# Output projection of a streaming encoder layer: whole-array matmuls split into an upper and a lower half of 64 rows

## The reference

```python
h = rms_norm(x, norm_pre)
p = h @ w_in                      # queries, keys, values, gates of three kinds of heads
o = concat(o_A * silu(g_A), o_B * silu(g_B), o_C * silu(g_C))   # "mixed", width 2048
y = x + rms_norm(o @ w_out, norm_post)   # w_out is 2048 x 2048
```

## Time and profile before

| | |
|---|---|
| median of three runs | 1939.62 us (1938.63 to 1939.85) |
| span of the profiled execution | 1936.8 us |
| the profiled execution's own time | not listed apart from the three |
| PE busy | 1905.3 us, 98% |
| DVE busy | 1240.0 us, 64% |
| ACT busy | 666.4 us, 34% |
| granted TensorE clock, mean | 0.997 |
| matmuls L1204 to L1206, 128x352 | 2688 each |
| matmuls L1400 to L1402, 128x512 | 448 each |
| matmuls L1396, L1397 | 64 each |

### The profile page before, as it was taken

The page is one execution under the profiler, slowest core; times in us unless marked ns, Lnnn a source line. Parts: engine busy times, 40 slices in busy tenths (PEclk is TensorE's granted clock), DMA queues, the critical chain, the costliest instruction groups (busy, mean ns, idle before and its releaser), DMA issues.

```text
span 1936.8 us, 30940 instructions
## 1 busy us (share of the span) xinstructions
PE 1905.3 (98%) x12508; PEld 1746.7 (90%) x12508; DVE 1240.0 (64%) x2224; ACT 666.4 (34%) x1257; POOL 53.3 (3%) x119
## 2 busy tenths in 40 slices
PE   6999999999999999999999999999999999999997
PEld 5999999999999999999999999999999988888886
DVE  7358777787878778553544454355525566766878
ACT  7124233343433334222222222233213354344453
POOL 4000000000000000000000000000000000000131
PEclk9999999999999999999999999999999999999999
DMA  6456777676777767666657667465446657555396
GB/s 245 117 120 137 159 157 165 145 147 154 146 162 154 162 146 149 151 137 136 149 119 155 141 136 143 104 141 123 106 97 144 136 197 278 192 175 187 121 258 226
DMA packets 880407, 301.05 MB, mean 155 GB/s; under 512 B 618504, under 2 KB 845592, under 8 KB 878968
## 3 DMA queue, kind: packets, MB, share of 16 engines
q1 hardware_dynamic: 877192, 290.35, 61.6%
q0 software_dynamic: 3072, 8.73, 2.2%
HBM read 210.45 MB, written 96.20 MB: 158 GB/s over the span
## 4 chain that ended last, share of the span: by engine, by line
PE 86%; DVE 9%; DMA 1%; ACT 1%; issue 1%; POOL 0%; SPq 0%; DVEq 0%; ACTq 0%; POOLq 0%
PE ps L1204 21%; PE ps L1205 20%; PE ps L1206 20%; PE ps L1400 4%; PE ps L1401 4%; PE ps L1402 4%; PE ps L1292 3%; PE ps L1371 3%; PE ps L1264 2%; PE ps L1342 2%; DVE arena L1853 1%; DVE act_lo L1740 1%; DVE arena L1733 1%; DMA b_out<-in_w_out_dram 1%; DVE arena L1841 1%
## 5 line engine op out<-in xcount | busy, mean ns | idle before, releaser
L1204 PE MATMUL ps<-act_hi,w_hi 128*128 128x352 f32 x2688 | 878.8, 327 | 0.1
L1206 PE MATMUL ps<-act_hi,w_lo 128*128 128x352 f32 x2688 | 863.7, 321 | 0.0
L1205 PE MATMUL ps<-act_lo,w_hi 128*128 128x352 f32 x2688 | 863.6, 321 | 0.0
L1204 PEld LDWEIGHTS ps<-act_hi,w_hi 128*128 128x128 f32 x2688 | 505.2, 188 | 24.7 <-issue 20.7
L1205 PEld LDWEIGHTS ps<-act_lo,w_hi 128*128 128x128 f32 x2688 | 506.1, 188 | 0.0
L1206 PEld LDWEIGHTS ps<-act_hi,w_lo 128*128 128x128 f32 x2688 | 504.9, 188 | 0.0
L1501 ACT ACTIVATE w_hi<-w_raw 128x512 fp32r<-128x512 f32 x224 | 139.3, 623 | 340.5 <-DMA w_raw<-in_w_in_dram 340.4
L1748 DVE TENSOR_TENSOR w_lo<-w_raw,w_hi 128x512 fp32r<-128x512 f32 x224 | 150.9, 675 | 51.5 <-ACT w_hi L1501 51.2
L1568 ACT ACTIVATE arena<-arena,small 128x257 f32<-128x257 f32 (+6 forms) x180 | 101.3, 565 | 209.1 <-DVE small L1891 209.1
L2079 DVE STREAM_TRANSPOSE arena<-arena 128x1024 f32<-128x1024 f32 (+4 forms) x100 | 132.6, 1326 | 40.0 <-ACT arena L1691 39.2
L1691 ACT ACTIVATE arena<-arena 128x1024 f32<-128x1024 f32 (+1 forms) x60 | 61.0, 1017 | 255.8 <-DVE arena L1865 255.7
(11 more groups left out here) (182 smaller groups left out, 2105.5 us busy)
## 6 DMA issues: line engine op xcount, KB each, us to landing
w_raw<-in_w_in_dram SPq DMA_DIRECT2D x176, 256.0 KB, 3.3
weight_scratch<-arena SPq DMA_DIRECT2D x216, 128.0 KB, 3.4
arena<-weight_scratch SPq DMA_DIRECT2D x54, 512.0 KB, 4.5
b_out<-in_w_out_dram SPq DMA_DIRECT2D x72, 256.0 KB, 3.3
w_raw<-in_w_out_dram SPq DMA_DIRECT2D x70, 256.0 KB, 2.7
w_raw<-in_w_in_dram SPq DMA_DIRECT2D x96, 128.0 KB, 3.1
weight_scratch<-arena SPq DMA_DIRECT2D x80, 132.0 KB, 4.1
arena<-weight_scratch SPq DMA_DIRECT2D x40, 256.0 KB, 3.3
```

Of the source, the lines that this page charges most:

```text
L1204: mm(bank(g, GN), wh, ah, start=(k == 0), stop=False)
L1205: mm(bank(g, GN), wh, al, start=False, stop=False)
L1206: last = mm(bank(g, GN), wl, ah, start=False, stop=(k == KT - 1))
```

## The change

Each matmul of the output projection, except in the last chunk, goes as two: one over rows 0 to 63 of the inner dimension, one over rows 64 to 127, both into the same bank and with the same 128 columns. They aren't issued one behind the other for the same group. `OUT` lists the groups in PE's order; `output(n)` issues, in turn, the upper-half matmuls of group n and the lower-half matmuls of group n - 2 (`OUT_LAG`). So the two halves in flight belong to different banks. A new semaphore `out_half` is incremented by the last upper-half matmul of a group, and the first lower-half matmul waits for it. `r_used` is now incremented by every group of a piece, with its last lower-half matmul, and two things wait for it: `wait_used`, for the last group of the piece, and the first upper-half matmul of a group, for the lower half of the same group in the piece before (`OUT_USED` holds the counts). Two more calls of `output` at the end issue the lower halves that are left. The tail keeps matmuls of 128 rows and its order.

```diff
+OUT = [(r, j) for r in range(LEAD) for j in range(3)] + [x for r in range(LEAD) for x in ((r, 3), (r, 4), (LEAD, r))]
+OUT += [(LEAD, 3), (LEAD, 4)] + [(r, j) for r in range(LEAD + 1, TAIL0) for j in range(GROUPS_IN[r // KH])]
+OUT_LAG = 2
+OUT_NO = {rj: n + 1 for n, rj in enumerate(OUT)}
+OUT_USED = dict(zip(OUT, itertools.accumulate(r % KH < KH - 1 for r, _ in OUT)))
...
-                eng.wait_ge(r_used, (KH - 1) * s + k + 1)
+                eng.wait_ge(r_used, OUT_USED[r, GROUPS_IN[s] - 1])
...
+            def out_free(r, j):
+
                 s, k = divmod(r, KH)
-                m, c = STAGE[s]
                 g = G0[s] + j
-                if k == 0 and g >= 8:
+                if k:
+                    if r < TAIL0:
+                        pe.wait_ge(r_used, OUT_USED[r - 1, j])
+                elif g >= 8:
...
+            def out_rows(r, j, x, rows, first, end):
+
+                s, k = divmod(r, KH)
+                out = bank((G0[s] + j) % 8)
                 if j == 4:
-                    if first:
-                        pe.wait_ge(ls_low, SAMPLE_OF[m] + 1)
-                    both = ls[SAMPLE_OF[m]][:, 2 * DEC * k:2 * DEC * k + P]
-                    mm(out, both, wh, start=first, stop=False)
-                    last = mm(out, both, wl, start=False, stop=end)
+                    still = ls[SAMPLE_OF[STAGE[s][0]]][rows, 2 * DEC * k:2 * DEC * k + P]
+                    moving = (r_hi(r), r_lo(r))[x][rows, :]
                 else:
-                    th, tl = l_hi[k][:, P * j:P * j + P], l_lo[k][:, P * j:P * j + P]
-                    mm(out, th, wh, start=first, stop=False)
-                    mm(out, th, wl, start=False, stop=False)
-                    last = mm(out, tl, wh, start=False, stop=end)
-                if end:
+                    still = (l_hi, l_hi, l_lo)[x][k][rows, P * j:P * j + P]
+                    moving = (r_hi(r), r_lo(r), r_hi(r))[x][rows, :]
+                return mm(out, still, moving, start=(first and k == 0 and x == 0),
+                          stop=(end and k == KH - 1 and x == (1 if j == 4 else 2)), skip_group_check=True)
+
+            def out_upper(r, j, x):
+                if x == 0:
+                    out_free(r, j)
+                last = out_rows(r, j, x, slice(0, 64), True, False)
+                if x == (1 if j == 4 else 2):
+                    last.then_inc(out_half, 1)
+
+            def out_lower(r, j, x):
+                if x == 0:
+                    pe.wait_ge(out_half, OUT_NO[r, j])
+                last = out_rows(r, j, x, slice(64, P), False, True)
+                if x == (1 if j == 4 else 2):
+                    last.then_inc(y_done if r % KH == KH - 1 else r_used, 1)
+
+            def output(n):
+
+                for x in range(3):
+                    if n < len(OUT) and x < (2 if OUT[n][1] == 4 else 3):
+                        out_upper(*OUT[n], x)
+                    if n >= OUT_LAG and x < (2 if OUT[n - OUT_LAG][1] == 4 else 3):
+                        out_lower(*OUT[n - OUT_LAG], x)
+
+            def tail_mm(r, j):
+                out_free(r, j)
+                for x in range(3):
+                    last = out_rows(r, j, x, slice(0, P), True, True)
+                if r == PIECES - 1:
                     last.then_inc(y_done, 1)
...
-            for r in range(LEAD):
-                for j in (3, 4):
-                    out_mm(r, j)
-            for r in range(LEAD, TAIL0):
-                operands_out(r)
-                for j in range(GROUPS_IN[r // KH]):
-                    out_mm(r, j)
+            for n in range(3 * LEAD, len(OUT)):
+                r, j = OUT[n]
+                if j == 0:
+                    operands_out(r)
+                output(n)
+            for n in range(OUT_LAG):
+                output(len(OUT) + n)
```

More of the change, by code:

```diff
@@ L788, in build @@
         tail_high, tail_low = sem("tail_high"), sem("tail_low")
-        r_summed, r_high, r_low, r_used = sem("r_summed"), sem("r_high"), sem("r_low"), sem("r_used")
+        r_summed, r_high, r_low, r_used, out_half = sem("r_summed"), sem("r_high"), sem("r_low"), sem("r_used"), sem("out_half")
         l_summed, l_high, l_low = sem("l_summed"), sem("l_high"), sem("l_low")
@@ L1375, in band_values @@
                 last.then_inc(pv_done, 1)
-            def out_mm(r, j):
+            def out_free(r, j):
                 s, k = divmod(r, KH)
-                m, c = STAGE[s]
                 g = G0[s] + j
-                if k == 0 and g >= 8:
+                if k:
+                    if r < TAIL0:
+                        pe.wait_ge(r_used, OUT_USED[r - 1, j])
+                elif g >= 8:
                     before = GROUP[g - 8]
@@ L1387, in out_mm @@
                         pe.wait_ge(c_added, ADDS_BY[before])
-                elif k == 0 and g < 3:
+                elif g < 3:
                     pe.wait_ge(proj_out, 3 * (TILES - 1) + g + 1)
-                out, wh, wl = bank(g % 8), r_hi(r), r_lo(r)
-                first, end = k == 0, k == KH - 1
-                if j == 4:
-                    if first:
-                        pe.wait_ge(ls_low, SAMPLE_OF[m] + 1)
-                    both = ls[SAMPLE_OF[m]][:, 2 * DEC * k:2 * DEC * k + P]
-                    mm(out, both, wh, start=first, stop=False)
-                    last = mm(out, both, wl, start=False, stop=end)
-                else:
-                    th, tl = l_hi[k][:, P * j:P * j + P], l_lo[k][:, P * j:P * j + P]
-                    mm(out, th, wh, start=first, stop=False)
-                    mm(out, th, wl, start=False, stop=False)
-                    last = mm(out, tl, wh, start=False, stop=end)
@@ L1403, in out_mm @@
-                if end:
+                if j == 4 and k == 0:
+                    pe.wait_ge(ls_low, SAMPLE_OF[STAGE[s][0]] + 1)
+            def out_rows(r, j, x, rows, first, end):
+                s, k = divmod(r, KH)
+                out = bank((G0[s] + j) % 8)
+                if j == 4:
+                    still = ls[SAMPLE_OF[STAGE[s][0]]][rows, 2 * DEC * k:2 * DEC * k + P]
+                    moving = (r_hi(r), r_lo(r))[x][rows, :]
+                else:
+                    still = (l_hi, l_hi, l_lo)[x][k][rows, P * j:P * j + P]
+                    moving = (r_hi(r), r_lo(r), r_hi(r))[x][rows, :]
+                return mm(out, still, moving, start=(first and k == 0 and x == 0),
+                          stop=(end and k == KH - 1 and x == (1 if j == 4 else 2)), skip_group_check=True)
@@ L1404, in out_mm @@
                     last.then_inc(y_done, 1)
-                elif j == GROUPS_IN[s] - 1:
-                    last.then_inc(r_used, 1)
             def operands_out(r):
@@ L1452, in _ @@
                     for j in range(3):
-                        out_mm(n, j)
+                        output(3 * n + j)
             pe.wait_ge(o_kept, kept_no(NU - 1, 2))
@@ L1470, in _ @@
                         operands_out(r)
-                    out_mm(r, j)
+                    tail_mm(r, j)
         @block.scalar
```

## The result

The changed kernel takes 1944.88 us (median of 6, 1944.25 to 1946.01), the kernel before 1939.04 us in the same measurement (1938.03 to 1939.85). The ratio is 1.0031, interval [1.002, 1.0043]: 5.8 us slower. The forecast was 1932.1 us with a range of 1928 to 1947, so the time lies in the range and on the other side of no change. It is the time of the first rival, the gap that stays in each half, 1945. 0.3% is small, but the interval keeps clear of 1.

What follows compares the result with a forecast made beforehand. PE bounds the kernel, with 13.3 ns per matmul carrying no columns. Gain 12.9 less self-waits 2.9 and release 1.3 is 8.7; 0.3 gained, 1.3 drain: 7.7, rounded to 7.5, giving 1932.1 us, range 1928 to 1947.

Steps and rivals of the forecast that it cites:

- the first rival: Output projection: 13.3 ns gap stays in each half, slot 226.7 ns, only costs of 5.5 us left, 1945; chance 0.29.
- the price of a slot: Output projection: one upper and one lower half side by side take 216 ns instead of 226.7.
- the sum's term of 10.7 ns a matmul: Saving per converted matmul; 1210 up to the release of piece 90 give 12.9 us.
- Halves at once: Output projection: upper and lower halves run together, starting 7 to 10 ns apart or half a slot.
- Loads into streaming rows: Output projection: a half's weights load into rows still streaming, so the load adds no time to a slot.
- the prediction's rival on this point: Loads cannot enter their own streaming rows: +107 ns a slot less 10.7, +128 us, 2067; chance 0.04.
- Self-waits: Lead pieces: upper halves wait for the lower half issued just before; eight of 0.32 us, three of 0.1, sum 2.9 us.
- Release: Groups finish two groups later, 1.3 us; covered except at piece 6 and the load starting DVE's chain; 1.3 us counted.
- Drain: Before the tail, six lower halves run alone with nothing above them, 1.3 us later.

Runs made afterwards that it cites:

- stream: PE alone, layer left out: 24 matmuls or sets per kind (types, rows, columns); rounded whole 512 columns 226.8 ns, bf16 216.0 ns.
- lag3: Changed kernel with pieces 0 to 3 whole in the old order and lower halves three groups behind (`OUT_LAG = 3`): 1999.17 us, ratio 1.031.
- whole_lead: Changed kernel, but pieces 0 to 3 stay whole in the old order, halves only in pieces 4 to 103: 1940.76 us, 1.0011 of the kernel before.
- late_release: Kernel before, no matmul split, but increments of r_used and y_done from piece 4 on come two groups later: 1941.13 us, ratio 1.0012.
- six_tail: Kernel before with six extra whole matmuls (1.36 us) just ahead of the tail: 1938.73 us beside 1938.71, ratio 1.0.
- stream2: PE alone, layer left out: rounded and bf16 matmuls mixed, and narrower weights; a round of one rounded and two bf16 takes 680 ns.
- stream3: PE alone, layer left out: rounds of 4 rounded and 8 bf16 matmuls take 2670 ns, rounds of 2 and 4 take 1345 ns.

## Why the prediction was wrong, step by step

**The step that failed** is the price of a slot: "I take 216 ns, 213.3 and the gap of the row-paired rows, since these are the only rows with this shape". Measured: 226.7. There were two kinds of nearest row, one with the shape and another type, one with the type and another shape, and I chose shape. No row and no run shows 216 ns for the rounded type: the 2.7 ns above 213.3 were my estimate from the fp32 pairs of the earlier trace rows, and the runs show 226.7 to 226.8 in its place. The earlier trace rows already held the answer for fp32: on the whole array its records come 109 to 110 ns apart at 128 columns, in halves some 0.11 us, so the half array had no part in the gap in the one type where both were to be seen. I had both rows and kept the value of the shape. With 226.7 the sum's term of 10.7 ns a matmul, 12.9 us of gain, becomes none. stream shows the same spacing with 128, 64 and 32 rows, and with shifted halves.

**Halves at once: right.** Starts 0.01 us apart, 0.39 us each. **Loads into streaming rows: right.** Weight loads of the changed kernel:

```profile
1700.38 0.18 PEld L1413 LDWEIGHTS ps<-r_extra_lo,l_hi 64*128 64x128 f32 x1
1700.39 0.18 PEld L1413 LDWEIGHTS ps<-w_lo,l_hi 64*128 64x128 f32 x1
```

They begin with the matmuls of 1700.38 and 1700.39 in the same rows, and the next matmuls follow at the usual distance, at 1700.61 and 1700.62. In the prediction's rival on this point the 93 ns a slot should be 96, 107 less 10.7, and the total 2072 for 2067; nothing hangs on it. The 107 is in no run; a matmul behind a wait, its load exposed, lasts 0.50 us here (1592.33) and not 0.39.

**Self-waits: right in kind, near in size.** 0.32 us was worked out for each of eight, 0.1 for three. The holes in the lead phase are 0.32 to 0.37, with one of 0.43, and three of 0.11: some 3.2 us for 2.9. In lag3 they are 0.37 to 0.44. Missing was something else of that phase: above a sample group of two matmuls a lower half of three runs its third slot alone, and the self-wait that follows keeps the halves from catching up. The timeline shows it:

```profile
1600.17 0.39 PE L1413 MATMUL ps<-w_lo,l_hi 64*128 64x512 f32 x1
1600.40 0.39 PE L1413 MATMUL ps<-w_hi,l_lo 64*128 64x512 f32 x1
1600.85 0.49 PE L1413 MATMUL ps<-w_hi,ls 64*128 64x512 f32 x1
```

At 1600.40 one half starts and none beside it. This happens three times, 3 x 0.227 = 0.7 us. The phase cost 4.0 us in all, and whole_lead gets it back.

**Release: right at the chain, wrong at the banks.** The load that starts DVE's chain was issued 6.71 us later than before at PE's 5.35: the 1.3 us forecast. PE's hole at 1889.88 lies behind it, since DVE's additions there free the bank. But "so 1.3 is covered" wasn't true of the evacuations. In stage 6's copies, ACT's queue tells why (timeline, after):

```profile
1758.55 0.63 ACT L1617 ACTIVATE r_extra_hi<-r_extra 128x512 fp32r<-128x512 f32 x1 [5.59 <-DMA r_extra<-in_w_out_dram]
1759.09 2.04 ACT L1655 ACTIVATE raw<-ps 128x512 f32<-128x512 f32 x4
```

Four copies stand in ACT's queue behind a high part whose load was slow: issued at 1749.76 it took 8.77 us, at a time when x is being copied to the output (DMA share 0.96 from 1749.70 to 1758.60). In the kernel before the same high part and copies came in time:

```profile
1752.98 0.63 ACT L1580 ACTIVATE r_extra_hi<-r_extra 128x512 fp32r<-128x512 f32 x1 [5.15 <-DMA r_extra<-in_w_out_dram]
```

Up to there PE is 3.7 us later and the high part 5.6: 1.36 for the release and 0.5 for the load, which took 8.28 us before. There the copies ended a little ahead of PE's need, here behind it. In the three traces with late release the wait follows this load one for one: 7.97, 8.77 and 9.21 us of load (whole_lead, after, late_release) go with 0.16, 0.96 and 1.41 us of wait. So its size varies with the execution. The prediction priced a load at its median of 3.3 us here. Bank waits cost 1.0 + 0.3 + 0.3 us in the changed kernel.

**Drain: wrong.** 1.3 us were put on the path. six_tail shows that the tail's first group isn't waited for until ACT's squares behind DVE's chain are through.

**The rival.** Its 5.5 us were 2.9 + 1.3 + 1.3, the last of them wrong; measured were 4.0 - 0.9 in the lead pieces, 1.6 at the banks and 1.1 at the chain, 5.8, and 0.6 of chance in that execution: 6.5 of the span, to the rounding. The -0.9 is chance too. It came out at 1945 by luck as well: the drain that isn't paid stands for the banks that are, and the 2.8 us from span to time were 1 us too many. The execution with the span of 1936.8 is listed in the record at 1938.63, 1.8 us above, and the changed kernel's time lies 1.7 above its span, which makes up for the 1.0 us that its span came out longer. That its mechanism is the right one is shown by stream and late_release, not by the number.

**A version that beats both** isn't among these. No split of rows of the rounded type gained anything per slot, and whole_lead, the best form of the change here, is still 0.11% behind.

## What to carry to other kernels

When the unseen operation has two neighbours in the trace, one of its shape and one of its type, look for a row that varies one of them alone before choosing; a stream of 24 matmuls on an idle core decides it in one run. Splitting a matmul over rows gave only concurrency here, and where the array was full there was none to win. If work is finished out of order by a lag, price every release that hangs on it by the slowest transfer in that stretch and not by the median, and look at the end whether anyone waits. And before a wait of 0.9 us that has gone is called a gain, look for it in a second trace of the unchanged part.

## What the runs showed of the hardware

A column takes 0.417 to 0.418 ns in bf16 (stream, stream2) and 0.419 in the rounded type (stream). A rounded fp32 matmul costs 12.5 to 14 ns above its columns at 0.4167 ns each, at 256 (119.5 ns a matmul), 352 (159.2), 384 (173) and 512 columns (226.7), with the same weights again (227) or new ones, and on 128, 64 or 32 rows (stream). bf16 costs 2.5 to 2.7 (216 at 512 columns). An fp32 matmul of 512 columns is two records of 429 ns (stream). A change between the rounded type and bf16 costs 11 to 19 ns at 512 columns (stream2, stream3). Two halves or four quarters of the rounded type do run at the same time, at the pace of one (226.8 and 227.2 ns). A matmul that waits for the one just before it costs 0.32 to 0.44 us on top of its slot (after, lag3).
